# Meta tokens last in the split x, a new place for the operand that moves through TensorE, two value tiles for the stream's keys, and the rotary key turned by transfers

## The reference

```python
cq, ckv, kpe, mq, mk, mv, mo, mi, mf, za, zb = split(h @ w_in)   # 4096 x 12360
ckv  = rmsnorm(ckv)                      # 512 wide; for the sample 128 cached rows are added
kpe  = rope(rmsnorm(kpe), pos)           # 64 wide, one rotary key for all heads
q    = rmsnorm(cq) @ w_q_up              # 16 heads of 128 + 64
k, v = split(ckv @ w_kv_up)              # 16 heads of 128 + 128
attn = softmax(q_nope k^T + q_pe kpe^T, chunk mask) @ v
ml_h = mlstm(mq, mk, mv, mi, mf, state)  # 4 heads, keys 256, values 512, chunkwise
y    = x + concat(attn * silu(za), sigmoid(mo) * rmsnorm(ml_h) * silu(zb)) @ w_out
```

## Time and profile before

| | us |
|---|---|
| median of 3 runs | 1992.43 (1991.45 to 1993.08) |
| profiled execution, its own time | 1992.86 |
| its span in the trace | 1991.1 |
| TensorE busy in the span | 1982.9 |
| TensorE's granted clock, mean | 0.999 of full speed |

### The profile page before, as it was taken

One profiled execution on the slowest core, in us unless ns is written; L12 is line 12 of the kernel. 1 busy time (PEld: TensorE's weight loads), 2 busy tenths in 40 slices (PEclk: granted clock), 3 DMA queues, 4 the chain that ended last, 5 costly groups with the idle time before them and its releaser, 6 DMA issues.

```text
span 1991.1 us, 36199 instructions
## 1 busy us (share of the span) xinstructions
PE 1982.9 (100%) x14750; PEld 1959.7 (98%) x14750; DVE 1253.1 (63%) x2470; ACT 910.0 (46%) x1806; POOL 192.4 (10%) x227
## 2 busy tenths in 40 slices
PE   9999999999999999999999999999999999999998
PEld 9999999999999999999999999999999999999998
DVE  7756677776576786868777555444555664444444
ACT  4564456565444444444444444444444553333333
POOL 0011143443200000000000000000000000000000
PEclk9999999999999999999999999999999999999999
DMA  9765443333465554646546555555555566666665
GB/s 243 203 187 156 115 121 117 100 110 117 122 179 147 150 172 131 180 128 181 162 141 171 170 168 168 169 170 169 170 169 169 170 186 192 193 193 193 193 193 142
DMA packets 219862, 323.87 MB, mean 163 GB/s; under 512 B 28316, under 2 KB 100864, under 8 KB 219696
## 3 DMA queue, kind: packets, MB, share of 16 engines
q1 hardware_dynamic: 216400, 318.35, 55.6%
q10 hardware_dynamic: 3296, 3.22, 0.5%
HBM read 310.69 MB, written 9.63 MB: 161 GB/s over the span
## 4 chain that ended last, share of the span: by engine, by line
PE 99%; DVE 0%; DMA 0%; ACTq 0%; ACT 0%; issue 0%
PE bank L1893 31%; PE bank L1896 30%; PE bank L1897 30%; PE bank L2159 1%; PE bank L2129 1%; PE bank L2055 1%; PE bank L2058 1%; PE bank L2057 1%; PE bank L2220 0%; PE bank L2246 0%; PE bank L2125 0%; PE bank L2126 0%; DMA xt<-in_meta_tokens_dram 0%; PE bank L2258 0%; PE bank L2073 0%; PE bank L2074 0%
## 5 line engine op out<-in xcount | busy, mean ns | idle before, releaser
L1227 DVE TENSOR_TENSOR wlo<-raw,whi 128x512 fp32r<-128x512 f32 (+1 forms) x1256 | 811.3, 656 | 678.9 <-ACT whi L815 668.8
L1893 PE MATMUL bank<-xsplit,whi 128*128 128x288 f32 (+2 forms) x4128 | 1216.0, 295 | 2.2 <-DVE xsplit L1251 1.9
L1897 PE MATMUL bank<-xsplit,wlo 128*128 128x288 f32 (+2 forms) x4128 | 1212.1, 294 | 0.0
L1896 PE MATMUL bank<-xsplit,whi 128*128 128x288 f32 (+2 forms) x4128 | 1211.9, 294 | 0.0
L815 ACT CAST whi<-raw 128x512 fp32r<-128x512 f32 (+1 forms) x1256 | 706.7, 576 | 950.9 <-PE bank L1897 908.3
L1893 PEld LDWEIGHTS bank<-xsplit,whi 128*128 128x128 f32 (+1 forms) x4128 | 773.2, 187 | 4.7 <-issue 3.4
L1896 PEld LDWEIGHTS bank<-xsplit,whi 128*128 128x128 f32 (+1 forms) x4128 | 773.2, 187 | 1.6 <-issue 1.0
L1897 PEld LDWEIGHTS bank<-xsplit,wlo 128*128 128x128 f32 (+1 forms) x4128 | 772.7, 187 | 0.0
L1893 PE MATMUL bank<-latents,whi 128*128 128x288 f32 (+1 forms) x352 | 112.8, 320 | 0.1
L1896 PE MATMUL bank<-latents,whi 128*128 128x288 f32 (+1 forms) x352 | 106.9, 304 | 0.0
L1897 PE MATMUL bank<-latents,wlo 128*128 128x288 f32 (+1 forms) x352 | 106.7, 303 | 0.0
(11 more groups left out here) (294 smaller groups left out, 1245.4 us busy)
## 6 DMA issues: line engine op xcount, KB each, us to landing
raw<-in_w_in_dram SPq DMA_DIRECT2D x313, 512.0 KB, 3.8
raw<-in_w_out_dram SPq DMA_DIRECT2D x128, 512.0 KB, 3.8
raw<-in_w_in_dram SPq DMA_DIRECT2D x142, 256.0 KB, 3.1
raw<-in_w_q_up_dram SPq DMA_DIRECT2D x48, 384.0 KB, 3.3
raw<-in_w_kv_up_dram SPq DMA_DIRECT2D x16, 512.0 KB, 3.7
xres<-in_x_prompt_dram SPq DMA_DIRECT2D x32, 128.0 KB, 3.7
xt<-in_x_prompt_dram SPq DMA_DIRECT2D x28, 128.0 KB, 4.9
out_dram<-ytok SPq DMA_DIRECT2D x28, 128.0 KB, 3.5
```

The lines of the kernel that those rows point to most:

```text
L1227: ins = tt(lo, src, hi.bitcast(f32), ALU.subtract)
L1893: ins = mm(out, w_hi, m_hi, start=start, stop=False, **kw)
L1896: mm(out, w_hi, m_lo, start=False, stop=False, **kw)
L1897: return mm(out, w_lo, m_hi, start=False, stop=stop, **kw)
```

## The change

1. In `xsplit` the meta tokens come last: 256 prompt, 32 sample, 16 meta. Every slice of x or of the mix starts at column 0. `ROW_GAP` is 67, so they all start at 96 + 268 = 364, place 108; `ROW_END` and the table's part `spare` keep the tiles behind where they were.
2. The evictions still need meta first in ckvf, nraw, mkT and mvT: VectorE writes ckvf and nraw in two instructions instead of one, and adds one copy of 16 columns to mkT and one to mvT for each mLSTM head (`ml_r` counts 6 a head instead of 4). ScalarE makes one more copy of 16 columns, of the row factor.
3. The rotary key is doubled and turned by six transfers from SBUF to SBUF on SyncE's queue, before the last q weights of the first pair are loaded; the matmuls with `dup` and `rot` and the copy to `kpr` go. Instead of one product with the sine there is one with the sine with signs and the rolled gain.
4. The second copy of the meta keys is now also in the latents (two VectorE copies and one product that zeroes 64 columns, at unit 4 of the first pair), and the value tiles start at columns 0, 128, 256 and 384. The sample's scores run over 176 keys instead of 192; seven transposes are left of eight; value tile 0 is multiplied with 256 queries instead of 288. ScalarE copies 288 columns of probabilities instead of 320, VectorE once 288 instead of 192 and 96.
5. Some semaphores are merged; the table of constants is 192 columns smaller.

```diff
@@ constants and tiles
-PROB = [(0, N_META + P), (256, C_SAMPLE), (560, NKX - 256)]
+PROB = [(0, N_META + P), (256, C_SAMPLE), (SAMPLE_AT + TAIL, NKX - C_SAMPLE)]
+V_AT = (0, P, 2 * P, 3 * P)
-ROW_GAP = 43
+ROW_GAP = 67
+ROW_END = 40
-        mhi, mlo = xhi_[:, :, N_META:NT], xlo_[:, :, N_META:NT]
+        mhi, mlo = xhi_[:, :, 0:NQ], xlo_[:, :, 0:NQ]
@@ SyncE, loads of the first pair
-            pair(U_PAIR // 2, 0)
+            def latent_rows(m):
+                if m == 4:
+                    sp.wait_ge(free[0], use("narrow", 0) + 1)
+                    for a in (0, 64):
+                        sp.dma_start(kpr[a:a + 64, :], nraw[0:64, :]).then_inc(kp_in, 16)
+                    for a in range(0, P, 32):
+                        z = 32 - a % 64
+                        sp.dma_start(rope2[a:a + 32, :], nraw[z:z + 32, :]).then_inc(kp_turn, 16)
+            pair(U_PAIR // 2, 0, latent_rows)
@@ VectorE
+                if k == 4:
+                    dve.wait_ge(ck_lo, KC)
+                    nc.vector.tensor_copy(ckhi_[:, :, NKV:NKX], ckhi_[:, :, 0:N_META]).then_inc(ck_meta, 1)
+                    nc.vector.tensor_copy(cklo_[:, :, NKV:NKX], cklo_[:, :, 0:N_META]).then_inc(ck_meta, 1)
+                    ts_(latents[:, ck_end:ck_end + V_PAD], con[:, 0:V_PAD], 0.0, None, ALU.mult).then_inc(ck_meta, 1)
                 if k == 7:
-                    dve.wait_ge(full[7], use("latent", 7, 1) + 1)
-                    tt(rope2[:, :], bank[7][:, 0:NT], sinT, ALU.mult).then_inc(free[7], 1)
+                    dve.wait_ge(kp_in, 32)
+                    dve.wait_ge(kp_turn, 64)
+                    stt(rope2[:, :], rope2[:, :], G[:, G_KT:G_KT + 1], c("turn"), ALU.mult, ALU.mult).then_inc(kp_c, 1)
@@ qk_scale
+                nc.vector.tensor_copy(mkT[:, :, 0:N_META], mkF[:, :, NQ:NT]).then_inc(ml_r, 1)
@@ TensorE, group
-                        skip = N_META if ct < queries else 0
-                        mc = slice(0, NQ) if mixed else slice(c0 + skip, NT)
-                        ins = mm3(bank[b0 + ct][:, skip:n], whi[:, k % HL_SLOTS, s], wlo[:, k % HL_SLOTS, s],
+                        n = NQ if c0 or ct < queries else NT
+                        mc = slice(0, n)
+                        ins = mm3(bank[b0 + ct][:, at:at + n], whi[:, k % HL_SLOTS, s], wlo[:, k % HL_SLOTS, s],
@@ TensorE, latent
-                if k == 1:
-                    pe.wait_ge(free[0], use("narrow", 0) + 1)
-                    fill("latent", 6)
-                    mm(bank[6][:, 0:NT], dup, nraw[:, :], start=True, stop=True).then_inc(full[6], 1)
-                    mm(bank[7][:, 0:NT], rope1[:, 0:P], kpr, start=True, stop=True).then_inc(full[7], 1)
@@ TensorE, scores, transposes, weighted
-                         (bank[5][0:WIDE, 0:NKX - 256], slice(SEQ, SEQ + WIDE), slice(256, NKX)))
+                         (bank[5][0:WIDE, 0:NKX - C_SAMPLE], slice(SEQ, SEQ + WIDE), slice(C_SAMPLE, NKX)))
-                tr(bank[6][:, 256:256 + WIDE], prob[0:WIDE, d + 176:d + 304], some)
-                tr(bank[6][:, 288:288 + WIDE], prob[0:WIDE, d + 48:d + 176], some).then_inc(full[6], 1)
+                tr(bank[6][:, 256:256 + WIDE], prob[0:WIDE, d + P:d + 2 * P], some).then_inc(full[6], 1)
-                tr(bank[7][0:48, 256:384], prob[:, b + 256:b + 304], ident)
-                tr(bank[7][0:48, 384:384 + WIDE], prob[0:WIDE, d:d + 48], some).then_inc(full[7], 1)
+                tr(bank[7][:, 192:320], prob[:, b + 2 * P:b + 3 * P], ident)
+                tr(bank[7][:, 320:320 + WIDE], prob[0:WIDE, d:d + P], some).then_inc(full[7], 1)
-                for t, q0, w, at in ((0, 0, 288, 0), (1, 64, 192, 320), (2, 192, 96, 512), (3, 256, 32, 288)):
+                for t, q0, w, at in ((0, 0, 256, 0), (1, 64, 192, 288), (2, 192, 96, 480), (3, 256, 32, 256)):
```

More of the change, by code:

```diff
@@ L137, in use @@
     return before[bank] + nth + i * uses[bank]
[L141 to L145, removed]
+G_X, G_QA, G_KVA, G_MLO, G_QN, G_KN, G_QR, G_KR, G_N0, G_QT, G_KT = 0, 32, 44, 48, 64, 65, 66, 67, 68, 76, 77
+G_ROWS = 78
+CONST_PARTS = [("ident", 128), ("squares", SQUARE), ("gains", G_ROWS), ("blockones", 128),
+               ("cos", NT), ("sin", NT), ("turn", NT),
+               ("rowmask", 4), ("spare", 47)]
 CONST_AT = {}
@@ L166, in shape_constants @@
         part("blockones")[64 * b:64 * b + 64, 64 * b:64 * b + 64] = 1.0
[L167 to L171, removed]
     pos = np.concatenate([np.arange(C_SAMPLE), N_META + PAST + np.arange(DEC)]).astype(np.float32)
@@ L176, in shape_constants @@
     part("sin")[:] = np.tile(np.sin(ang), (4, 1))
-    part("turn")[:] = np.where(np.arange(P)[:, None] % 64 < 32, -1.0, 1.0) * part("sin")[:, N_META:]
+    part("turn")[:] = np.where(np.arange(P)[:, None] % 64 < 32, -1.0, 1.0) * part("sin")
     part("rowmask")[:, 0:2] = 1.0
@@ L204, in gain_columns @@
         t[0:64, at] = t[64:P, at] = np.asarray(inputs[name])
-    t[:, G_QT] = np.roll(t[:, G_QR].reshape(2, 64), 32, axis=1).reshape(P)
+    for at, own in ((G_QT, G_QR), (G_KT, G_KR)):
+        t[:, at] = np.roll(t[:, own].reshape(2, 64), 32, axis=1).reshape(P)
     return t
@@ L249, in c @@
             return con[0:rows, a:a + w]
-        ident, blockones, rot, dup = c("ident"), c("blockones"), c("rot"), c("dup", 72)
+        ident, blockones = c("ident"), c("blockones")
         cosT, sinT, G = c("cos"), c("sin"), c("gains")
@@ L1453, in first_pair @@
                     q_evict("bulk0", 0, 0)
[L1454 removed]
+                    dve.wait_ge(full[6], use("latent", 6, 1) + 1)
                     dve.wait_ge(ck_out, 32)
@@ L1910, in group @@
             def group(u, phase, nth, i, c0, hooks=lambda k: None, a_hi=xhi, a_lo=xlo, ready=None,
-                      queries=0, b0=0, turn=(0, 2, 1, 3), mixed=False, last=0):
-                n = NT - c0
+                      queries=0, b0=0, turn=(0, 2, 1, 3), last=0):
+                at = 0 if c0 else N_META
                 for k in range(KT - last):
@@ L1964, in row_sums @@
                     fill("rms", 4)
-                    mm(bank[4][:, 0:NT], ones, diag[:, X_PAD:], start=True, stop=True).then_inc(full[4], 1)
+                    mm(bank[4][:, 0:NT], ones, diag[:, 0:NT], start=True, stop=True).then_inc(full[4], 1)
             group(2 * KT, "cq", 0, 0, N_META, row_sums)
@@ L2053, in kv_units @@
                         out = bank[b][0:m, 256 * half:256 * half + 256].rearrange("p (h c) -> p h c", h=2)
-                        cs = slice(c0, c0 + m)
-                        mm(out, ckhi[:, k, cs], vcols(whi), start=k == 0 and half == 0, stop=False,
+                        v_hi = latents[:, ck_at + k * CK_ROW + c0:ck_at + k * CK_ROW + c0 + m]
+                        v_lo = latents[:, ck_rest + k * CK_ROW + c0:ck_rest + k * CK_ROW + c0 + m]
+                        mm(out, v_hi, vcols(whi), start=k == 0 and half == 0, stop=False,
                            skip_group_check=True)
-                        mm(out, cklo[:, k, cs], vcols(whi), start=False, stop=False, skip_group_check=True)
-                        ins = mm(out, ckhi[:, k, cs], vcols(wlo), start=False, stop=last, skip_group_check=True)
+                        mm(out, v_lo, vcols(whi), start=False, stop=False, skip_group_check=True)
+                        ins = mm(out, v_hi, vcols(wlo), start=False, stop=last, skip_group_check=True)
                         if last and half == 1:
```

167 lines of the change are left out of this document (85 added, 82 removed).

## The result

The changed kernel takes 2014.73 us (2013.93 to 2015.24, four runs), the kernel before, on the same chip, 1992.49. The ratio is 1.0112, 95% interval 1.0100 to 1.0123: 22 us slower, where 11 us faster was predicted, and outside the range.

What follows compares the result with a forecast made beforehand. TensorE, busy 1982.9 of 1991.1 us, was taken as the bound. Savings of 7.6 (304 wide), 1.0 (rotary key) and 2.5 (attention), 11.1 us in all, took 1992.4 to 1981.3 us; range 1962 to 1993.

Steps and rivals of the forecast that it cites:

- 288 wide, from place 76 to 108: 9600 matmuls on x or the mix: no difference, 130.0 ns each; bounds 19 us gained to 48 us lost.
- rival C: 288 columns cost more at place 108: 1990.9 us at +1 ns, 2010.1 at +3 ns; chance 0.15.
- The rule of lines of 16 bytes: SBUF reads of x: places 12, 76 and 108 lie alike in a line, so 7.6 us less gain.
- 304 wide, from place 12 to 108: 2688 matmuls in ckv and mLSTM groups: the extra at place 12 goes, to 136.7 ns, saving 7.6 us.
- rival B: The place of x does nothing, 304 columns stay at 140.0 ns: 1988.9 us; chance 0.16.
- The small parts: Rotary key's matmuls and attention on TensorE: 1.0 and 2.5 us gained, 3.5 us together.
- the value tile: Attention: value tile 0 loses 32 columns in two passes, saving 0.85 us.
- the transposes: Attention, 16 heads: one transpose of 72 columns goes in each, saving 1.0 us.
- the scores: Attention: the sample's scores lose 16 columns, saving 0.43 us in fp32 products and 0.2 in float32r ones.
- the rotary key's two matmuls: Matmuls with `dup` and `rot` go on TensorE, saving 0.52 and 0.51 us, together 1.0 us.
- Rival E: Transfers on SyncE make TensorE wait in the first pair: 1982 to 1984 us; chance 0.05.

Runs made afterwards that it cites:

- run 3: Changed kernel with the split weights 32 bytes on, at place 160, and x still at 108: 1991.91 us.
- run 5: Changed kernel with row pairs of x going through sixteen places in steps of 16 bytes, weights at 128: 1999.94 us.
- run 6: Changed kernel with row pairs of x going through sixteen places in steps of 16 bytes, weights moved to 160: 1999.01 us.
- run 7: Changed kernel with both moved 32 bytes on, weights at 160 and x at 140: 2013.76 us.
- run 1: Changed kernel with x and the mix at place 76 instead of 108, all else kept: 1991.4 us, ratio to the kernel before 0.9995.
- run 2: Kernel before with x 32 bytes on, 288 columns at place 108 and 304 at 44: 2025.11 us.
- run 9: Kernel before with only x moved, 304 columns at place 236 and 288 at 44: 1988.10 us, ratio 0.9978.
- run 8: Changed kernel with x and the mix at place 124 instead of 108: 1983.62 us, ratio to the kernel before 0.9955.
- run 4: Changed kernel with rows of x 321 columns apart instead of 320, so places advance in steps of 4 bytes: 2021.81 us.

## Why the prediction was wrong

**The step that failed** is "*288 wide, from place 76 to 108*", with "I take no difference, 130.0". It measured 133.3 ns, and by the sums 29.5 us in place of 0. That is more than everything else in the prediction together, and it is rival C, "288 columns cost more at place 108", almost at its second price (+3 ns, 2010.1 us). The place was named as the largest unknown and bounded at -19 to +48 us. But the value taken rested on rows whose stationary operand lies elsewhere. In the kernel before, the constant that lines 1976 and 1977 hold stationary lies at place 96, so their differences are 0 and +128, and -96 and +32: none is -20. The prediction ordered these rows by x's place alone. Runs 3, 5, 6 and 7 show that x's place alone doesn't give the cost.

**The reason for not looking at the weights' place.** The prediction gave a rule of the Trainium skill (SBUF — State Buffer, "Who interferes with whom"): weights and moving data are read through separate ports, so nothing should hang on where one lies against the other. It was noted that no row separates the two. The measurement goes against what I drew from it: with x untouched, moving the weights by 32 bytes changes the distance from 133.3 to 130.0 (run 3), and moving both by 32 bytes restores it (run 7). Two ports may still exist; what they read isn't independent. The rule of lines of 16 bytes, by which 12, 76 and 108 are alike, is also not the whole of it: the sweep in steps of 16 bytes goes from 130.0 to 136.7.

**304 wide, from place 12 to 108.** The term was 7.6 us and measured 6.4: the long stretches went from 140.0 to 136.7, the value read behind a break in the earlier trace rows. That it was the place that did this is shown (run 1 takes it back, run 7 brings it again), so rival B is out. The reasoning was only half right, though, and the size is in part luck. The prediction laid the extra to place 12 because the 288 wide matmuls at place 76 don't have it. But at 304 columns place 76 has it too (run 1), and so has 44 (run 2): it belongs to the width and the difference together. That 108 is free of it at this width no row could tell, just as none could tell that it is dear at the other.

**The small parts** were 3.5 us and measured 2.5: 3.0 and 0.3 saved, less 0.85 lost. That loss is a term that I didn't have. The products for v, where the weights move and the key tile is stationary, went from a mean of 118.5 ns (45.49 us by 384) to 120.7. It goes with the new value tiles: the mean is 118.1 to 118.5 in the kernel before and in runs 9 and 2, and 120.7 to 121.1 in the changed kernel and in runs 1 and 8. The tiles' places differ in one point: before, a quarter of the stationary tiles began at place 12 and the others at 76, and in the new layout all begin at 76. That alone doesn't explain it, for the matmuls of the three quarters that stayed at 76 also went from 118.2 to 120.3 ns. The cause stays open. Of the estimates for attention, the value tile saved 0.86 us (0.85 predicted), the transposes 1.1 (1.0) and the scores 0.4 (0.6); the rotary key's two matmuls saved 1.0 as predicted, a part of it in the row of `latents`, and the matmuls of line 1964 cost 0.2 more.

**Rival E** (transfers on SyncE make TensorE wait) is out by the row of line 2102 above and the distances behind it: no wait.

**The range** ended at 1993 because it took in only the mildest part of C, though the bound of +5 ns stood beside it. An operand that 9600 matmuls share, at 9.6 us a nanosecond and with no row at its new place, deserved more than the 0.15 that C got, and the range should have reached to C at +3 ns. With four of sixteen differences over 132 ns, one that was not looked up is dear in about one case of four.

**The sum that would have been right**: 1992.4 + 29.5 - 6.4 - 0.3 + 0.85 - 3.0 = 2013.1, against 2014.7 measured (2013.9 in the profiled execution, from which the terms come).

## What to carry to other kernels

When a layout change moves an operand that TensorE streams thousands of times, ask where it will lie modulo 256 against the stationary operand, and try the places (16 bytes apart) before pricing anything else; a sweep inside one kernel, with blocks of rows at successive places, does it in one run. Confirm the place it names with all rows there: at 288 columns the sweep held (130.1 ns and 130.0 at -4, 132.8 and 133.3 at -20), at 304 it did not at -20. Read start-to-start distances, not durations, and take a neighbouring row as evidence only if all of its operands lie as those of the case do. Empty words are a tuning knob of their own: the same kernel ran 2014.7, 1991.4 and 1983.6 us with gaps of 67, 59 and 71 words.

## What the runs showed of the hardware

- The steady distance of 288 wide float32r matmuls depends on the moving operand's place less the stationary one's, modulo 256. With the weights at a multiple of 16 and x at 12 modulo 16, it is 130.0 to 130.5 ns at nine of sixteen differences, but 133.3 at -20 and 136.7 at +124 (runs 5 and 6); at the other places of x modulo 16 the mean is higher (run 4). Shifting both operands by 32 bytes, the only shift tried, leaves it unchanged (run 7, and sixteen places in runs 5 and 6).
- All steady distances of long stretches with x at a fixed place and both weight tiles at one stand 3.3 ns apart: 130.0 and 133.3 at 288 columns, 136.7 and 140.0 at 304. A cost of less than that was only ever seen as a mean over blocks or places.
- The width counts as well: at the difference -20, 288 columns are one step above their floor and 304 are at the lowest value seen; at -52 it is the other way round (runs 1, 3 and 7).
- At the difference +108, 304 columns run at 136.7 in some stretches and at 140.0 in others, in one execution (run 9).
- The clock was full in all of these (granted 0.998 to 1.000), and VectorE and ScalarE were as busy as before (1252 to 1254 us and 909 to 911 us).
